# Reading the cached keys behind the whole in-projection, with the page chunks issued by SyncE and GpSimd

## The reference

```python
proj = (h @ w_in).astype(jnp.float32)          # w_in: 1024 x 2048
q, k, v = jnp.split(proj, [nqd, nqd + nkd], axis=-1)
q = partial_rope(q.reshape(b, L, ATT_HEADS, HEAD_DIM), pos)
k = partial_rope(k.reshape(b, L, KV_HEADS, HEAD_DIM), pos)
...
k_all = jnp.concatenate([k_past.astype(jnp.float32), k], axis=1)   # sample group only
v_all = jnp.concatenate([v_past.astype(jnp.float32), v], axis=1)
o = moba_attend(q, k_all, v_all, pos)
y = o.reshape(b, L, nqd).astype(h.dtype) @ w_out
```

## Time and profile before

| | |
|---|---|
| median of three runs | 1899.84 us |
| the profiled execution | 1897.98 us, span 1896.1 us |
| mean granted TensorE clock | 0.949 of full speed |
| TensorE matmul busy | 1734.7 us, 91% of the span |
| VectorE, ScalarE, GpSimd busy | 1288.5, 985.2, 74.6 us |
| transfers | 529.27 MB, mean 279 GB/s |

### The profile page before, as it was taken

The page is one execution under the profiler, slowest core; times in us unless marked ns, Lnnn a source line. Parts: engine busy times, 40 slices in busy tenths (PEclk is TensorE's granted clock), DMA queues, the critical chain, the costliest instruction groups (busy, mean ns, idle before and its releaser), DMA issues.

```text
span 1896.1 us, 26994 instructions
## 1 busy us (share of the span) xinstructions
PE 1734.7 (91%) x9800; PEld 1455.8 (77%) x9800; DVE 1288.5 (68%) x1410; ACT 985.2 (52%) x940; POOL 74.6 (4%) x98
## 2 busy tenths in 40 slices
PE   5999988899998973887999999999999999999993
PEld 4788886899998831365888888888888888888882
DVE  5874673555544631114798888989889888898882
ACT  3542230444433331002777777777777777777770
POOL 1340000000000000001000000000000000000000
PEclk9998898999999996886999999999999999999996
DMA  7322123454446799873799999999999999999962
GB/s 294 112 73 113 68 112 144 153 181 178 179 155 237 229 358 387 328 290 135 307 370 363 400 378 381 371 374 388 380 381 370 360 404 364 388 375 371 391 266 59
DMA packets 100942, 529.27 MB, mean 279 GB/s; under 512 B 11305, under 2 KB 11498, under 8 KB 48114
## 3 DMA queue, kind: packets, MB, share of 16 engines
q1 hardware_dynamic: 82592, 482.72, 66.5%
q10 hardware_dynamic: 13970, 25.46, 3.7%
q0 software_dynamic: 4288, 19.90, 3.4%
HBM read 513.38 MB, written 14.65 MB: 278 GB/s over the span
## 4 chain that ended last, share of the span: by engine, by line
PE 82%; DVE 7%; issue 3%; ACTq 2%; ACT 2%; DMA 2%; SPq 1%; POOL 0%; POOLq 0%; DVEq 0%
PE bank L1010 16%; PE bank L1012 16%; PE bank L1011 16%; PE bank L518 6%; PE bank L519 6%; PE bank L520 6%; PE bank L759 3%; ACTq L423 1%; PE bank L1047 1%; PE bank L630 1%; PE bank L927 1%; ACTq L421 1%; PE bank L675 1%; DVE ring L1676 1%; DVE w_lo L1507 1%
## 5 line engine op out<-in xcount | busy, mean ns | idle before, releaser
L1899 DVE TENSOR_TENSOR w_lo<-raw_w,w_hi 128x2048 fp32r<-128x2048 f32 x336 | 768.7, 2290 | 115.5 <-ACT w_hi L1306 113.5
L1306 ACT ACTIVATE w_hi<-raw_w 128x2048 fp32r<-128x2048 f32 x336 | 644.8, 1920 | 338.9 <-PE bank L1012 247.6
L1010 PE MATMUL bank<-w_hi,xe_hi 128*128 128x512 f32 x896 | 353.9, 395 | 1.8 <-DVE xe_lo L1962 1.8
L1012 PE MATMUL bank<-w_hi,xe_lo 128*128 128x512 f32 x896 | 349.9, 391 | 0.0
L1011 PE MATMUL bank<-w_lo,xe_hi 128*128 128x512 f32 x896 | 349.5, 390 | 0.0
L519 PE MATMUL bank<-fh_lo,w_hi 128*128 128x264 f32 x704 | 201.6, 286 | 0.0
L1012 PEld LDWEIGHTS bank<-w_hi,xe_lo 128*128 128x128 f32 x896 | 168.7, 188 | 36.0
L1010 PEld LDWEIGHTS bank<-w_hi,xe_hi 128*128 128x128 f32 x896 | 168.8, 188 | 35.8 <-issue 1.8
L1011 PEld LDWEIGHTS bank<-w_lo,xe_hi 128*128 128x128 f32 x896 | 169.0, 189 | 34.0
L1010 PE MATMUL bank<-w_hi,aT_hi 128*128 128x512 f32 x448 | 176.7, 394 | 0.0
L1012 PE MATMUL bank<-w_hi,aT_lo 128*128 128x512 f32 x448 | 174.7, 390 | 0.0
(11 more groups left out here) (355 smaller groups left out, 2252.1 us busy)
## 6 DMA issues: line engine op xcount, KB each, us to landing
raw_w<-in_moe SPq DMA_DIRECT2D x336, 1024.0 KB, 6.3
raw_w<-in_ffn_w SPq DMA_DIRECT2D x42, 1024.0 KB, 4.8
ring<-in_k_pages SPq DMA_DIRECT2D x96, 256.0 KB, 3.7
raw_w<-in_gdn_in SPq DMA_DIRECT2D x16, 1024.0 KB, 6.6
ring<-in_v_pages SPq DMA_DIRECT2D x64, 256.0 KB, 11.6
ring<-in_v_pages ACTq DMA_DIRECT2D x64, 256.0 KB, 11.1
ring<-in_att_in SPq DMA_DIRECT2D x4, 2048.0 KB, 7.8
ring<-in_k_pages ACTq DMA_DIRECT2D x32, 256.0 KB, 7.6
```

The source lines that it names most:

```text
L1010: mm(out, hi, move_hi, start=first, stop=False)
L1012: return mm(out, lo, move_hi, start=False, stop=last)
L1306: A(w_hi[:, p % SPLIT, :], raw_w[:, p % RAW, :], ACT.Copy).then_inc(split_hi, 1)
L1899: V.tensor_tensor(w_lo[:, p % SPLIT, :], raw_w[:, p % RAW, :], w_hi[:, p % SPLIT, :].bitcast(F32), ALU.subtract).then_inc(split_lo, 1)
```

## The change

Page chunks are issued by chunk: SP issues every even one whole, POOL every odd one whole, ACT none. POOL issues the K/V store after key chunk 15. POOL has completion semaphores of its own (`pages_full`). Odd chunks take the slots in another order (`slot_of`): key chunk 7 takes slot 5, and key chunk 9 slot 3, which the last in-projection weights leave.

The key chunks 0 to 3 are read by TensorE right behind the last column chunk of the in-projection, ahead of head 0; then each head's turn reads two chunks (4 and 5 with head 0, ..., 14 and 15 with head 5). Since key scores take banks 0 to 3 earlier, the in-projection's results go to banks 6 and 7 only, and TensorE waits from column chunk 2 on for the copy of the chunk before last. `q_wide` gets memory of its own (`q_home`), cleared beside column chunk 1 and filled behind column chunk 8's rotation; to make room, the weight ring has three units in place of four, and `aproj` counts halves. ACT splits the next weights before it copies a result, and asks for the rotary table before the first split. The semaphores of the softmax chain are merged into three.

```diff
-ATT_UNITS = 4
+ATT_UNITS = 3
+Q_WIDE_N = NS * 130 + P
...
+ODD_CYCLE = (3, 7, 1, 5)
+def slot_of(n):
+    k = n - C_K
+    if 6 < k and k % 2 == 1 and n < C_AOUT:
+        return 5 if k == 7 else ODD_CYCLE[(k - 9) // 2 % 4]
+    return 6 if n == C_AOUT + 1 else n % SLOTS
+def slot_before(n):
+    return max(m for m in range(n) if slot_of(m) == slot_of(n))
+def by_pool(n):
+    return C_K <= n < C_AOUT and n % 2 == 1
...
-        def load_pages(eng, n, pages):
+        def load_pages(eng, n):
             first, cache = (C_K, k_pages) if n < C_V else (C_V, v_pages)
             slot_free(eng, n)
-            for page in pages:
+            for page in range(PPC):
...
-            for n in range(C_K, C_AOUT):
-                load_pages(sp, n, range(0, PPC) if n < C_BOTH else range(0, PPC // 2))
+            for n in range(C_K, C_AOUT, 2):
+                load_pages(sp, n)
...
+            KEYS_BESIDE = {15: (0, 1, 2, 3)}
             for c in range(16):
-                if c >= 4:
-                    pe.wait_ge(aproj_sb, c - 3)
+                if c >= 2:
+                    pe.wait_ge(aproj_sb, c - 1)
...
-                    last = stationary_mm(bank[c % 4][:, 0:T], hi, lo, ...)
-                last.then_inc(aproj, 1)
+                    last = stationary_mm(bank[6 + c % 2][:, 0:T], hi, lo, ...)
+                    if k % 4 == 3:
+                        last.then_inc(aproj, 1)
                 if 1 <= c <= 12:
                     rotate(c - 1)
+                for key in KEYS_BESIDE.get(c, ()):
+                    if key == 0:
+                        pe.wait_ge(q_set, Q_WIDE)
+                    key_chunk(key)
...
             for i in range(H + 2):
...
-                if i == 0:
-                    pe.wait_ge(q_wide_set, 1)
-                key_chunk(i)
-            for c in range(H + 2, 2 * NS):
-                key_chunk(c)
-                if c == 2 * NS - 2:
-                    pe.wait_ge(prod_done, 1)
-                    pe.wait_ge(pT_sb, H)
-                    mm(bank[6][:, 0:1], prodn, ones[:, 0:1], start=True, stop=True).then_inc(lnew_ps, 1)
+                for key in range(4 + 2 * i, min(6 + 2 * i, 2 * NS)):
+                    key_chunk(key)
+            pe.wait_ge(q_set, Q_PROD)
+            pe.wait_ge(pT_sb, H)
+            mm(bank[6][:, 0:1], prodn, ones[:, 0:1], start=True, stop=True).then_inc(softmax_ps, 1)
...
                 if n == 0:
                     act.wait_ge(f_used, PIECES)
+                    act.dma_start(rope, rope_in).then_inc(prm_loaded, 16)
                 if n >= ATT_UNITS:
-                    act.wait_ge(aproj, c - 1)
+                    act.wait_ge(aproj, n - ATT_UNITS + 1)
...
             for c in range(16):
-                act.wait_ge(aproj, c + 1)
-                if c == 0:
-                    act.dma_start(rope, rope_in).then_inc(prm_loaded, 16)
-                A(aq[:, c, :], bank[c % 4][:, 0:T], ACT.Copy).then_inc(aproj_sb, 1)
                 for n in range(2 * c + ATT_UNITS, min(2 * c + ATT_UNITS + 2, 32)):
                     split_a(n)
+                act.wait_ge(aproj, 2 * c + 2)
+                A(aq[:, c, :], bank[6 + c % 2][:, 0:T], ACT.Copy).then_inc(aproj_sb, 1)
...
-                if i >= 1:
-                    load_pages(act, C_BOTH + i - 1, range(PPC // 2, PPC))
-            for n in range(C_BOTH + H + 1, C_V + SLOTS):
-                load_pages(act, n, range(PPC // 2, PPC))
...
-            for n in range(C_V + SLOTS, C_AOUT):
-                load_pages(act, n, range(PPC // 2, PPC))
...
-            pool.wait_ge(roped, 12)
-            pool.wait_ge(aproj_sb, 16)
-            pool.dma_start(kv_out, aq[:, 8:16, :]).then_inc(stored, 16)
+            pool.wait_ge(table_loaded, 16)
+            for n in range(C_K + 1, C_AOUT, 2):
+                load_pages(pool, n)
+                if n == C_V - 1:
+                    pool.wait_ge(roped, 12)
+                    pool.wait_ge(aproj_sb, 16)
+                    pool.dma_start(kv_out, aq[:, 8:16, :]).then_inc(stored, 16)
...
+                if c == 1:
+                    V.memset(q_home, 0.0)
+                    V.tensor_reduce(mod32, ident.rearrange("p (k m) -> p m k", m=32), AX, ALU.add)
+                if c == 8:
+                    dve.wait_ge(roped, 8)
+                    V.tensor_copy(q_own.rearrange("p b k r -> p k r b"), ...).then_inc(q_set, 1)
             dve.wait_ge(roped, 12)
+            V.tensor_tensor(prod_own, ...).then_inc(q_set, 1)
```

More of the change, by code:

```diff
@@ L108, in fills_per_chunk @@
     return 16 * (PPC if C_K <= n < C_AOUT else 1)
+ODD_CYCLE = (3, 7, 1, 5)
[8 more added lines that the diff above has]
+    return C_K <= n < C_AOUT and n % 2 == 1
 def full_value(n):
-    return sum(fills_per_chunk(m) for m in range(n % SLOTS, n + 1, SLOTS))
+    return sum(fills_per_chunk(m) for m in range(n + 1) if slot_of(m) == slot_of(n) and by_pool(m) == by_pool(n))
 CST = {}
@@ L333, in program @@
         ring_full = [sem(f"ring_full{s}") for s in range(SLOTS)]
+        pages_full = {s: sem(f"pages_full{s}") for s in range(1, SLOTS, 2)}
         x_loaded, prm_loaded, lmask_loaded = sem("x_loaded"), sem("prm_loaded"), sem("lmask_loaded")
@@ L484, in load_expert @@
                         slot = p * PIECE // SLOT
-                        last = max(n for n in range(CHUNKS) if n % SLOTS == slot)
+                        last = max(n for n in range(CHUNKS) if slot_of(n) == slot)
                         sp.wait_ge(v_read, last - C_V + 1)
@@ L815, in rotate, with key_chunk @@
                 mm(bank[4 + c % 2][0:ROT, 0:T], rot_p, aq[:, c, :], start=True, stop=True).then_inc(rot_ps, 1)
+            def key_chunk(c):
+                n, b = C_K + c, c // 2
+                arrived(n)
+                keys = ring[:, slot_of(n), :].rearrange("p (q g h t) -> p q g h t", q=2, g=4, h=KVH)
+                for q in range(2):
+                    for h in range(KVH):
+                        last = mm(bank[2 * (c % 2) + q][32 * h:32 * h + 32, :].rearrange("p (g t) -> p g t", t=PAGE),
+                                  q_wide[:, KVH * b + h, :], keys[:, q, :, h, :],
+                                  start=(b == 0), stop=(b == NS - 1), skip_group_check=True)
+                last.then_inc(k_read, 1)
+            KEYS_BESIDE = {15: (0, 1, 2, 3)}
             for c in range(16):
-                if c >= 4:
-                    pe.wait_ge(aproj_sb, c - 3)
+                if c >= 2:
+                    pe.wait_ge(aproj_sb, c - 1)
                 for k in range(KT):
@@ L905, in _ @@
                 if g % 8 == 7:
-                    last.then_inc(probT_ps, 1)
-            mm(bank[7][:, 0:64], ones, p_diag, start=True, stop=True).then_inc(probT_ps, 1)
+                    last.then_inc(softmax_ps, 1)
+            mm(bank[7][:, 0:64], ones, p_diag, start=True, stop=True).then_inc(softmax_ps, 1)
             def turn_o(b):
@@ L1792, in _ @@
             rest_of_input(KT - 1, 2)
-            for n in range(2, ATT_UNITS):
-                rest_of_att(n)
+            rest_of_att(2)
             def turn_heads(c):
@@ L1851, in _ @@
                     p_max(i)
-            dve.wait_ge(lnew_ps, 1)
+            dve.wait_ge(softmax_ps, LNEW_PS)
             V.tensor_copy(l_new, bank[6][:, 0:1])
```

91 lines of the change are left out of this document (41 added, 50 removed).

## The result

The kernel with the change took 1904.84 us (median of 20 runs, 1900.33 to 1909.84), the kernel before 1900.31 us beside it (20 runs): ratio 1.0019, 95% interval 1.0011 to 1.0028. So it is slower, by some 4 us; 1892 had been forecast, with 1884 to 1911 as the range. The profiled execution has a span of 1904.4 us against 1896.1, and a mean granted clock of 0.938 against 0.949. The in-projection's column weights were issued 2.3 us later in this execution than in that of before (596.42 against 594.08), for reasons that lie ahead of the change. The two profiled executions thus lie 8.3 us apart where the medians lie 4.5 apart.

What follows compares the result with a forecast made beforehand. Bound: the attention stage's bytes at 387 GB/s plus time the DMA engines are not full. Last landing 806.2 + 1.5 = 807.7 against 814.0, 6.3 gained (in-projection's 1.3 within), taken as 6: 1897.98 - 6 = 1892 us, range 1884 to 1911.

Steps and rivals of the forecast that it cites:

- (a): In-projection: two result banks and three weight units cost nothing; the earlier rope table request gains net 1.3 us.
- (b): Page transfers: DMA engines full from 662.5 us, 55.6 MB at 387 GB/s take 143.7 us, ending at 806.2.
- Rival 2: Mixed SP and POOL queues carry 5% under 387 GB/s: +7.6 us, no gain, 1899 us; chance 15%.
- rival 3: Page transfers beat the forecast, 55.6 MB at 413 GB/s: 9.1 us less, 1883 us; chance 15%.
- (c): Softmax: last key chunk near 719 us, new-token product at about 732, values begin at 753, not 761.4.
- the hole: Transfer stall at 760 us, all slots holding unreadable values: 4.2 + 2.4 us of full-rate time, forecast about 1.5.
- (d): Stage end: last landing at 807.7 us against 814.0, 6.3 gained; the 5.9 us to the out-projection stays.
- (e): POOL's cost per page: taken as 1.05 us, under the 1.355 at which it keeps its half.
- The rivals that end slower or level: POOL becomes the bound above 1.36 us a page, 1913 us, 20%; mixed queues carry less, 1899 us, 15%.

## Why the prediction was wrong

**(a) In-projection: right.** Two banks and three units cost nothing: TensorE is busy 35.00 of 35 us. The first key chunk follows at 661.53, 65.1 us behind the issue of the column weights; before, the in-projection ended 66.8 behind it. 1.6 were gained, 1.3 forecast.

**(b) The sum of bytes: right, but begun too early.** From 664.5 to the last value landing at 817.5 are 153 us and 54.78 MB, 0.8 MB less than summed up; at 387 GB/s they are 141.6 us, and the idle from 665 to 675, 1.9, and behind 680, 9.9, make 153.4. Rival 2 is out (388 GB/s at a share of 1.04) and so is rival 3. What the text took too lightly is the start: counting from 662.5 hides that nothing moves from 656 to 664. In the sum of idle that is 11.5 against 7.2 of before, but not all of it is lost. What had been moved from 590 to 680, first before the change, then after it:

```profile
DMA packets 10997, 22.81 MB, mean 253 GB/s; under 512 B 1213, under 2 KB 1213, under 8 KB 10732
```
```profile
DMA packets 9024, 22.22 MB, mean 247 GB/s; under 512 B 1218, under 2 KB 1218, under 8 KB 8886
```

By 655 the changed kernel was 1.1 MB ahead (16.99 against 15.91), by 680 it is 0.59 MB behind: a loss of 1.5 us, in an execution that began 2.3 us later.

**(c) The softmax: the step that failed.** "Values begin at 753", "the hole shrinks to about 1.5": 764.43 and 9.9. The landing of the last key (719 forecast, 721.5 measured, in an execution that began 2.3 us later) came out by luck: nine key chunks and the store from 662.5 on are 20.0 MB, in by 714 at 387 GB/s. In the trace 21.22 of a possible 22.8 MB were moved from 662.5 to 721.5, since nothing moved at first (4.2 us), and some 1.2 MB of these were values that GpSimd's queue brought ahead of SP's last keys (3.1 us). From there:
- The last pair was to be read by 721; it was read from 721.58 to 728.08. SP's chunk, the late one, is the first of the two, so both stand behind its landing, mostly at half clock (6.50 us for two chunks that take 3.64 at full). 7.1 later in all, 2.3 of it the later start.
- "Heads 6 and 7 follow, each with the 4.64 us", then 1 us: from 721 to about 732. It was 15.6 us to the new-token product (728.1 to 743.7). The 4.64 came from head 0 in the earlier trace rows, at full clock and in a loop with work between; the turns here are 5.36 and 6.16 us, and there are three heads' probabilities to turn, not two: head 5's had waited behind the pair as well. 4.6 later.
- From the product to the first value 20.7 measured, 21 forecast. Right, and the removed wait of ScalarE with it.

7.1 + 4.6 - 0.3 = 11.4, as found. The first value came 11.4 us later than forecast, and the hole was 8.4 larger. Undoing the pairs alone took the whole hole away and brought the out-projection 9.5 us forward; 1.9 of these lay ahead of the in-projection in that execution, and by the medians it is 10.9.

**(d) The tail.** 8.1 us from the last landing to the out-projection, not 5.9: it is SP's even chunk again, so two chunks are read behind it, 2.90 us for the first and 1.92, at full clock again, for the second, with the turning between. Here the assumption of equal shares failed; "the merged semaphores and the slot order I cost at nothing" held for the slot order in the changed kernel, where plain slots gave 1907.30; the semaphores no run tested.

**(e) GpSimd's page: right.** 1.14 us against 1.05 taken, no bound. The table load took 288 ns there (median of 128), not 508, and no issue of its key pages took over 578 ns, those beside VectorE's operations included. At five pages in eight its lane was the late one, in a kernel some 21 us slower than the one before.

In sum, against the forecast, which had the out-projection at 813.6 (807.7 + 5.9): it came at 825.56, 12.0 later. The transfers began at 664.5 and not at 662.5 (2.0), stood idle at 665 to 675 (1.9) and had 0.8 MB less to move (-2.1); the hole was 8.4 larger and the tail 2.2 longer; 0.4 is left over. The hole, and with it step (c), is most of it. Against the kernel before: idle 6.9 us larger, everything else 1.3 smaller, and the out-projection 5.6 later. Of the 8.3 us between the two spans, 2.6 come behind the start of the out-projection, and no run explains them. The rivals that end slower or level looked at the queues; their uneven share is real, but most of the loss was in the order of TensorE's own work.

## What to carry to other kernels

Where a stage is bound by transfers, its time is bytes over rate plus every gap in the stream; ask of each reordering first whether the buffers can run full in it, at the start as well as at the end. A chain of short rounds between engines should be spread so that each round hides behind one arrival; packing the arrivals in twos leaves rounds over at the end, uncovered and at the lower clock. When a step is priced from a row, count how many of them remain at that point in the new order, and take the duration from a row in the same state of the clock.

## What the runs showed of the hardware

- Two hardware queues with 256 KB pages share the engines evenly (3.84 and 3.85 MB in 20 us), GpSimd's software queue and a hardware queue 59 to 41 (4.57 and 3.16 MB), with packets of 3.3 and 1.8 KB. With SP's larger rows (5.2 KB a packet) it turns to 35 to 65 (5.60 and 10.61 MB in 40 us).
- A page issued by GpSimd takes 1.14 us with a table load, about as long as on SP (1.15 before the change, 1.10 from 664 to 690 behind it); the engine is busy 0.55 of it, and the issue took 546 to 578 ns in all 64 key pages, also beside VectorE's maxima and scalings in the heads' turns.
- With TensorE waiting 3.4 us of each round, the granted clock of the stretch 740 to 760 is 0.50, the lower of its two levels (1.2 GHz), and a turn takes 6.2 to 6.9 us in place of 5.3; 32 key products took 6.50 us at 721 and 3.64 at full clock.
